# Loading a head's query weights as 88 and 40 partitions instead of 128

## The chip, the core and the metric

The kernel runs on one core of one Trainium2 chip. The metric is device time of one execution in microseconds (us). The core has TensorE (PE), VectorE (DVE), ScalarE (ACT), GpSimd (POOL) and a SyncE queue (SP), and 16 DMA engines that move data between HBM and the on-chip memory of 128 partitions.

## What is computed

One layer of a streaming encoder for 512 prompt frames and 32 sample frames of width 1024: RMSNorm, a projection, retention and a gated convolution, an output projection, and then PEER, a layer of single-neuron experts. In PEER, each of 8 heads asks for 16 of 16384 experts for every frame:

```
qry = (xb @ peer_query).reshape(P, PEER_HEADS, 2, PEER_KEY_DIM)
scores = einsum('phsd,hsnd->phsn', qry, keys)       # 128 keys in each of two halves
top_s, top_i = top_k(scores, 16)                    # then the best 16 of 16 x 16 sums
expert = (ia * PEER_KEYS + ib)                      # 16 experts a frame and head
u_rows = peer_down[expert]; v_rows = peer_up[expert]
act = gelu(einsum('pd,ped->pe', xb, u_rows))
out = einsum('pe,ped->pd', gate * act, v_rows)
```

The rows of `peer_down` and `peer_up` lie side by side in one table, `experts`, of 8 KB a row. The outputs are the final-normed frames and the retention and convolution states.

## The kernel before, in words

Everything is float32. The first 340 us hold the mixers (projection, convolution, retention); after them, and partly beside them, runs the PEER part, to which this change belongs.

PEER is cut into 34 steps, `vt`: four tiles of 128 frames for each of 8 heads, and two last steps in which the 32 sample frames are folded over the 128 partitions. Each step has 16 gathers, 544 in all. A gather (L601) is an indirect DMA that POOL issues: for each of 128 partitions one row of 8 KB, 1 MB in all, into one of 12 slots of `arena`. DVE waits for the slot's semaphore and takes the dot product of the first half of the rows with the frame (L1313); ACT makes of it the gelu and the weight (L895, L898) and a diagonal matrix (L909); PE multiplies the second half of the rows by it and sums in PSUM (L1674, for the sample L1667). When PE has used a slot, POOL may issue the gather that comes 12 later. So two things can hold the stream: the DMA engines, and the ring of 12 slots through DVE, ACT and PE.

Every gather's semaphore reaches its full count only when all DMA engines that carry a part of it have told of the end of theirs.

The weights of a head are 128 partitions of 2304 floats (queries and sub-keys), 1152 KB. They lie in two buffers in turn, `head_flat[head % 2]`, each with a semaphore (`s_hw`). Heads 0 and 1 are loaded earlier (L480, L491). A loop on SP loads heads 2 to 7 (L502 to L504): for head 2 it waits for PE's last scores of head 0, for each later one for the projections two heads back. PE asks for them in `later_query` (L1633), about one head before the head's own gathers. The order of work on each engine is written out; no scheduler is involved.

Of the kernel before, what the change touches and what calls it, by code (L numbers as in the profile page):

```python
# [14 lines left out]
P = 128  # L15
# [42 lines left out]
def shape_constants():  # L58

    f = np.float32  # L60
    half = HD // 2
    inv = (f(10000.0) ** (-np.arange(half, dtype=f) / f(half))).astype(f)
    pos = np.concatenate([np.arange(SEQ, dtype=f), f(PAST) + np.arange(DEC, dtype=f)])
    ang = (pos[:, None] * inv[None, :]).astype(f).astype(np.float64)
    trig = np.zeros((P, TILES, 2, half), f)
    for t in range(TILES):
        r = ROWS[t]
        trig[:r, t, 0] = np.cos(ang[t * P:t * P + r])
        trig[:r, t, 1] = np.sin(ang[t * P:t * P + r])
    log_gamma = np.log1p(-np.exp2(-5.0 - np.arange(HEADS)))  # L70
    i = np.arange(P)
    diff = i[None, :] - i[:, None]
    scale = HD ** -0.5
    decay = np.zeros((P, HEADS, P), f)
    cross = np.zeros((P, HEADS, P), f)
    key_decay = np.zeros((P, 2, HEADS), f)
    for h in range(HEADS):
        decay[:, h] = np.where(diff >= 0, np.exp(log_gamma[h] * np.maximum(diff, 0)), 0.0) * scale
        cross[:, h] = np.exp(log_gamma[h] * (i + 1.0))[None, :]
        key_decay[:, 0, h] = np.exp(log_gamma[h] * (P - 1.0 - i)) * scale  # L80
        key_decay[:DEC, 1, h] = np.exp(log_gamma[h] * (DEC - 1.0 - i[:DEC])) * scale
    ident = np.eye(P, dtype=f)
    fold = (np.arange(P)[:, None] % DEC == np.arange(P)[None, :]).astype(f)
    iota = np.broadcast_to(np.arange(TOPK, dtype=f), (P, TOPK))
    parts = [trig.reshape(P, -1), decay.reshape(P, -1), cross.reshape(P, -1), key_decay.reshape(P, -1),
             ident, fold, iota]
    return np.concatenate(parts, axis=1).astype(f)
# [33 lines left out]
def plan():  # L121
# [34 lines left out]
    def glu(s, *parts):  # L156
        return [("glu", s, c, i) for c, i in parts]
# [22 lines left out]
def parts(vt):  # L180

    steps = [range(g * GROUP, (g + 1) * GROUP) for g in range(GROUPS)]
    return steps if vt < VT - 1 else steps[:-1] + [range(k, k + 1) for k in steps[-1]]

def named(text):
# [39 lines left out]
def steps(vt, g):  # L226

    rows = parts(vt)[g]
    return [rows[i:i + 2] for i in range(0, len(rows), 2)]
# [9 lines left out]
def build(nc, x_prompt, x_sample, x_turned, state_ret, conv_state, weights, head_weights, params, consts, gain_ffn, gain_final,  # L239
          experts, y_prompt, y_sample, ret_prompt, ret_sample, conv_prompt, conv_sample):  # L240
    ctx = ExitStack()
    with ctx:
# [3 lines left out]
        def sem(name):  # L246
            return ctx.enter_context(nc.semaphore(name))
# [33 lines left out]
        head_flat = [region_b[:, first_at:first_at + HEAD_W + 2 * KEYS], region_b[:, 0:HEAD_W + 2 * KEYS]]  # L281
# [92 lines left out]
        s_hw = [sem("s_hw_even"), sem("s_hw_odd")]  # L374
# [59 lines left out]
        def _(sp):  # L434
# [64 lines left out]
            for head in range(2, PH):  # L499
                if head == 2:  # L500
                    sp.wait_ge(s_pe, JOB[("scores", SAMPLE)] + 1)
                else:  # L502
                    sp.wait_ge(s_proj, (head - 2) * PROJ)
                sp.dma_start(head_flat[head % 2], head_weights[head]).then_inc(s_hw[head % 2], 16)  # L504
            last = VT * TOPK - 1
            sp.wait_ge(s_slot[SLOT[last]], slot_filled(last))
            for t in range(SAMPLE):
# [965 lines left out]
        def _(pe):  # L1473
# [149 lines left out]
            def later_query(head, i):  # L1623

                weights = head_w[head % 2][0]
                if head == 1:
                    before = BEFORE_QUERIES[i]
                    pe.wait_ge(s_by[BY[before[0]]], EMPTIED[before])
                elif i < 3:
                    pe.wait_ge(s_scored, (head - 2) * 3 + (i + 1))  # L1630
                else:
                    pe.wait_ge(s_queries, (head - 1) * PIECES)
                pe.wait_ge(s_hw[head % 2], 16 * (head // 2 + 1))  # L1633
                s, half = i // 2, i % 2
                for k in range(KD):
                    last = mm(ps[:, Q_BANKS + i, 0:HALF], weights[:, k, s * KEYS:(s + 1) * KEYS],  # L1636
                              hT[:, k, half * HALF:(half + 1) * HALF], start=k == 0, stop=k == KD - 1)
                last.then_inc(s_proj, 1)
# [48 lines left out]
            def next_head(head, m):  # L1687

                if m == 0:
                    return {g: lambda g=g: later_query(head + 1, g) for g in range(PIECES)}  # L1690
                if m == 1:
                    return {2: lambda: later_scores(head + 1)}
                return {}

            for step in PLAN:
# [29 lines left out]
                else:  # L1725
                    sum_up(step[1], step[2])

            later_query(1, 0)
            later_query(1, 1)
            sum_up(2, 0)  # L1730
            later_query(1, 2)
# [81 lines left out]
```

## Time and profile before

| | us |
|---|---|
| median of 3 runs | 1667.71 (1667.13 to 1667.92) |
| the profiled execution | 1667.42 |
| its span, first to last instruction | 1665.6 |
| DVE busy | 1225.5 |
| PE busy | 1109.6 |
| POOL busy | 680.6 |
| ACT busy | 572.6 |
| SP loads of heads 2 to 7, issued | 344.0 to 1006.6 |

The profile's page gives busy times, the span in 40 slices, the DMA queues (q0 is POOL's, q1 SP's, q8 and q14 carry instructions), and the chain of work that ended last. The timeline gives single instructions with the idle time before them in brackets and what ended it. No view tells the 16 DMA engines apart.

### The profile page before, as it was taken

What the parts mean: (1) busy time and instruction counts of PE and PEld (TensorE: products, weight loads), DVE (VectorE), ACT (ScalarE), POOL (GpSimd) and SP (SyncE); (2) the same over time, 40 slices, a digit from 0 to 9 for tenths busy, and PEclk for the clock granted to TensorE, in tenths of its full rate; (3) what the DMA queues carried; (4) which work ended last, traced back from release to release, by engine and by line L of the source; (5) the groups of instructions that cost most, each with busy time, mean ns of one, the idle gap of its engine ahead of it and who ended that gap; (6) DMA issues with size and microseconds to landing.
All of it is one profiled execution on the core that took longest, in us unless ns stands there. A gap on an engine that the chain in (4) does not pass through costs nothing.

```text
span 1665.6 us, 19298 instructions
## 1 busy us (share of the span) xinstructions
PE 1109.6 (67%) x6327; PEld 464.1 (28%) x6327; DVE 1225.5 (74%) x2651; ACT 572.6 (34%) x1785; POOL 680.6 (41%) x633
## 2 busy tenths in 40 slices
PE   7999999785675567556654665567667656665533
PEld 6744465441231122112211221122113211111111
DVE  3997858976877777677767777777777777777755
ACT  2212232532333333333333333334333333333342
POOL 0004634544443444444344433444444444444552
PEclk9999999887897778877978887798768876767755
DMA  7203227999999999999999999999999999999995
GB/s 292 102 1 98 111 83 293 371 420 421 421 421 421 421 421 422 421 421 420 421 421 422 421 420 421 421 420 422 419 417 419 420 416 421 419 417 419 420 421 239
DMA packets 88004, 608.73 MB, mean 365 GB/s; under 512 B 11104, under 2 KB 13664, under 8 KB 16224
## 3 DMA queue, kind: packets, MB, share of 16 engines
q0 software_dynamic: 78336, 570.46, 82.8%
q1 hardware_dynamic: 9568, 37.04, 6.0%
q8 instruction: 50, 0.82, 0.2%
q14 instruction: 50, 0.41, 0.1%
HBM read 604.19 MB, written 2.88 MB: 364 GB/s over the span
## 4 chain that ended last, share of the span: by engine, by line
DMA 47%; PE 23%; DVE 17%; issue 5%; POOL 4%; DVEq 2%; ACT 2%; ACTq 0%; SPq 0%; POOLq 0%
DMA arena<-experts,expert 46%; PE ps L1536 8%; PE ps L1674 8%; DVE arena L1313 7%; PE ps L1516 4%; POOL arena L601 4%; DVE xs L1334 4%; DVEq L1250 1%; ACT late L909 1%; DVE rot_tmp L1273 1%; DVE codes L1251 1%; ACT weight L898 1%; DVE top_s L1254 1%; DVE top_s L1249 1%; PE ps L1495 1%
## 5 line engine op out<-in xcount | busy, mean ns | idle before, releaser
L1674 PE MATMUL ps<-arena,late 64*64 64x512 f32 x4032 | 663.5, 799 | 480.6 <-ACT late L909 480.4
L601 POOL DMA_INDIRECT arena<-experts,expert x544 | 609.0, 1119 | 772.8 <-PE ps L1674 648.5
L1313 DVE CUSTOM_DVE_ANT_0 arena<-arena,hn 128x1024 f32<-128x1024 f32 x544 | 651.0, 1222 | 311.0 <-DMA arena<-experts,expert 307.4
L1674 PEld LDWEIGHTS ps<-arena,late 64*64 64x64 f32 x4032 | 173.9, 172 | 944.0 <-ACT late L909 696.3
L895 ACT ACTIVATE gl<-dots 128x2 f32<-128x2 f32 (+1 forms) x274 | 55.8, 204 | 810.3 <-DVE dots L1313 810.3
L909 ACT ACTIVATE late<-cst,weight 128x128 f32<-128x128 f32 (+1 forms) x536 | 183.6, 389 | 18.9 <-issue 0.3
L898 ACT ACTIVATE weight<-gl,gate 128x1 f32<-128x1 f32 x544 | 130.8, 287 | 19.5 <-issue 0.7
L1536 PE MATMUL ps<-arena,hT 128*128 128x512 f32 x256 | 111.1, 593 | 0.0
L1636 PE MATMUL ps<-hT,region_b 128*128 128x272 f32 x448 | 110.8, 401 | 0.0
L1064 DVE SCALAR_TENSOR_TENSOR region_b<-region_b,par 128x574 f32<-128x574 f32 x120 | 92.6, 813 | 4.5
L1636 PEld LDWEIGHTS ps<-hT,region_b 128*128 128x128 f32 x448 | 83.8, 192 | 39.3 <-issue 23.5
L1334 DVE TENSOR_TENSOR xs<-ps,xs 64x512 f32<-64x512 f32 x128 | 88.0, 688 | 2.3
L1536 PEld LDWEIGHTS ps<-arena,hT 128*128 128x128 f32 x256 | 48.2, 190 | 58.1 <-issue 58.1
L1667 PE MATMUL ps<-arena,late 128*32 128x256 f32 x256 | 30.1, 611 | 47.8 <-ACT late L909 47.8
L1536 PE MATMUL ps<-arena,region_b 128*128 128x512 f32 x128 | 56.5, 595 | 2.5 <-issue 2.5
L551 POOL TENSOR_TENSOR rot_tmp<-arena,cst 128x512 f32<-128x512 f32 (+1 forms) x5 | 6.3, 1266 | 125.4 <-DVE hn L1212 125.0
L1313 DVE DVE_READ_ACCUMULATOR2_ANT dots<- 128x1 f32 x544 | 44.8, 82 | 0.0
L871 ACT ACT_TABLE_LOAD x33 | 42.3, 1283 | 1.7
L895 ACT ACT_TABLE_LOAD x32 | 41.1, 1283 | 0.6
L1516 PE MATMUL ps<-hn,arena 128*128 128x272 f32 x160 | 36.8, 392 | 0.0
L1536 PEld LDWEIGHTS ps<-arena,region_b 128*128 128x128 f32 x128 | 23.8, 190 | 31.0 <-issue 30.9
L1516 PEld LDWEIGHTS ps<-hn,arena 128*128 128x128 f32 x160 | 30.4, 190 | 6.3
(174 smaller groups left out, 853.4 us busy)
## 6 DMA issues: line engine op xcount, KB each, us to landing
arena<-weights SPq DMA_DIRECT2D x6, 2048.0 KB, 10.9
region_b<-head_weights SPq DMA_DIRECT2D x8, 1152.0 KB, 9.4
arena<-experts,expert POOLq DMA_INDIRECT x544, 23.0
hT<-x_turned SPq DMA_DIRECT2D x2, 1088.0 KB, 7.2
arena<-weights SPq DMA_DIRECT2D x4, 512.0 KB, 10.7
xs<-x_prompt SPq DMA_DIRECT2D x4, 512.0 KB, 10.0
arena<-weights SPq DMA_DIRECT2D x2, 1024.0 KB, 13.8
y_prompt<-xs SPq DMA_DIRECT2D x4, 512.0 KB, 3.8
```

Of the source, the lines that this page charges most:

```text
L601: pool.indirect_dma_start(rows_of(n), None, experts, bass.IndirectOffsetOnAxis(ap=expert[:, vt % BUFS, k:k + 1], axis=0))\
L871: nc.scalar.activation(gate[:, u, :], best_s[:, u, :], ACT.Exp, bias=neg_max[:, u:u + 1], accum_out=gate_sum[:, u:u + 1]).then_inc(s_exp, 1)
L895: nc.scalar.activation(gl[:, vt % 2, ks], dots[:, vt % 2, ks], ACT.Gelu_apprx_tanh)
L898: ready = nc.scalar.activation(weight[:, vt % 2, k:k + 1], gl[:, vt % 2, k:k + 1], ACT.Copy, scale=gate[:, vt % BUFS, k:k + 1])
L909: nc.scalar.activation(diag[:, n % DIAGS, 0:base.shape[-1]], base, ACT.Copy, scale=weight[:, vt % 2, k:k + 1])\
L1064: return v.scalar_tensor_tensor(out=conv[:, c, :], in0=u[:, c, j:j + WIDE], scalar=gain, in1=conv[:, c, :], op0=ALU.mult, op1=ALU.add)
L1313: last = v.tensor_tensor_reduce(out=rows_of(n)[:, 0:D], in0=rows_of(n)[:, 0:D], in1=hn[:, tile_of(vt)], scale=1.0, scalar=0.0, op0=ALU.mul ...
L1334: last = v.tensor_tensor(out=part, in0=total, in1=part, op=ALU.add)
L1516: last = mm(out[:, 0:HALF], w[:, c, k, :], columns[:, k, i * HALF:(i + 1) * HALF], start=k == 0, stop=k == KD - 1)
L1536: last = mm(out, lhs[:, k, lo:lo + r], w[:, k, :], start=k == 0, stop=k == KD - 1)
L1636: last = mm(ps[:, Q_BANKS + i, 0:HALF], weights[:, k, s * KEYS:(s + 1) * KEYS], hT[:, k, half * HALF:(half + 1) * HALF], start=k == 0, sto ...
L1674: last = mm(ps[half * TOKENS:(half + 1) * TOKENS, 2 * (vt % 2) + i, :], diag[tokens, n % DIAGS, tokens], rows_of(n)[tokens, D + half * SEC ...
```

## The change

A list of partition ranges per head is put in: heads 2, 3 and 4 have two, 0 to 87 and 88 to 127, all others one. SP issues one transfer for each range, and the wait of PE counts 16 for each. The same bytes go to the same places.

```diff
+def head_rows(head):
+
+    return [slice(0, 88), slice(88, P)] if 2 <= head < 5 else [slice(0, P)]
+
+
+def head_filled(head):
+
+    return 16 * sum(len(head_rows(h)) for h in range(head % 2, head + 1, 2))
...
-                sp.dma_start(head_flat[head % 2], head_weights[head]).then_inc(s_hw[head % 2], 16)
+                for rows in head_rows(head):
+                    sp.dma_start(head_flat[head % 2][rows], head_weights[head][rows]).then_inc(s_hw[head % 2], 16)
...
-                pe.wait_ge(s_hw[head % 2], 16 * (head // 2 + 1))
+                pe.wait_ge(s_hw[head % 2], head_filled(head))
```

On SP's queue, from the copies of the sample frames to the stores of the output, this stood before (the size is partitions x floats):

```order
L494 DMA hn<-hn 32x1024 [waits s_hn]
L494 DMA hn<-hn 32x1024 x2
L495 DMA region_b<-gain_final 128x1024
L497 DMA var<-gain_final 32x256 x4
L504 DMA region_b<-head_weights 128x2304 [waits s_pe]
L504 DMA region_b<-head_weights 128x2304 [waits s_proj] x5
L509 DMA y_prompt<-xs 128x1024 [waits s_yout,s_slot7]
```

And this stands there now:

```order
L504 DMA hn<-hn 32x1024 [waits s_hn]
L504 DMA hn<-hn 32x1024 x2
L505 DMA region_b<-gain_final 128x1024
L507 DMA var<-gain_final 32x256 x4
L515 DMA region_b<-head_weights 88x2304 [waits s_pe]
L515 DMA region_b<-head_weights 40x2304
L515 DMA region_b<-head_weights 88x2304 [waits s_proj]
L515 DMA region_b<-head_weights 40x2304
L515 DMA region_b<-head_weights 88x2304 [waits s_proj]
L515 DMA region_b<-head_weights 40x2304
L515 DMA region_b<-head_weights 128x2304 [waits s_proj] x3
L520 DMA y_prompt<-xs 128x1024 [waits s_yout,s_slot7]
```

Three transfers have become six, each second one issued right behind its first; the waits stand where they stood. On PE, DVE, ACT and POOL every instruction keeps its place.

## Rows read from the trace of the kernel before

**Rows 1.** The page: span, DVE, the 40 slices of DMA, the queues.

```profile
span 1665.6 us, 19298 instructions
...
DVE  3997858976877777677767777777777777777755
...
DMA  7203227999999999999999999999999999999995
GB/s 292 102 1 98 111 83 293 371 420 421 421 421 421 421 421 422 421 421 420 421 421 422 421 420 421 421 420 422 419 417 419 420 416 421 419 417 419 420 421 239
...
q0 software_dynamic: 78336, 570.46, 82.8%
...
q8 instruction: 50, 0.82, 0.2%
q14 instruction: 50, 0.41, 0.1%
```

**Rows 2.** The page's chain that ended last, by engine.

```profile
DMA 47%; PE 23%; DVE 17%; issue 5%; POOL 4%; DVEq 2%; ACT 2%; ACTq 0%; SPq 0%; POOLq 0%
```

**Rows 3.** All waits: who waited for whom, us, times, the longest.

```profile
POOL arena L601 <- PE ps L1674: 648.5, 314, 8.3
...
DVE arena L1313 <- DMA arena<-experts,expert: 307.4, 247, 3.7
```

**Rows 4.** DMA issues: count, KB each, median us from issue to landing.

```profile
region_b<-head_weights SPq DMA_DIRECT2D x8, 1152.0 KB, 9.4
arena<-experts,expert POOLq DMA_INDIRECT x544, 23.0
```

**Rows 5.** Timeline of DVE near 1056 us: start, duration, instruction, [idle before].

```profile
1053.58 1.23 DVE L1313 CUSTOM_DVE_ANT_0 arena<-arena,hn 128x1024 f32<-128x1024 f32 x1 [1.19 <-DMA arena<-experts,expert]
...
1056.06 1.23 DVE L1313 CUSTOM_DVE_ANT_0 arena<-arena,hn 128x1024 f32<-128x1024 f32 x1 [1.25 <-DMA arena<-experts,expert]
...
1058.54 1.23 DVE L1313 CUSTOM_DVE_ANT_0 arena<-arena,hn 128x1024 f32<-128x1024 f32 x1 [1.25 <-DMA arena<-experts,expert]
```

**Rows 6.** Timeline of DVE, five dot products around the longer steps.

```profile
492.17 1.23 DVE L1313 CUSTOM_DVE_ANT_0 arena<-arena,hn 128x1024 f32<-128x1024 f32 x1 [2.28 <-DMA arena<-experts,expert]
...
1105.72 1.23 DVE L1313 CUSTOM_DVE_ANT_0 arena<-arena,hn 128x1024 f32<-128x1024 f32 x1 [0.89 <-DMA arena<-experts,expert]
...
1109.18 1.23 DVE L1313 CUSTOM_DVE_ANT_0 arena<-arena,hn 128x1024 f32<-128x1024 f32 x1 [2.22 <-DMA arena<-experts,expert]
...
1230.32 1.23 DVE L1313 CUSTOM_DVE_ANT_0 arena<-arena,hn 128x1024 f32<-128x1024 f32 x1 [2.23 <-DMA arena<-experts,expert]
...
1583.80 1.23 DVE L1313 CUSTOM_DVE_ANT_0 arena<-arena,hn 128x1024 f32<-128x1024 f32 x1 [2.26 <-DMA arena<-experts,expert]
```

**Rows 7.** Timeline of DVE while the weights of head 5 come in.

```profile
679.15 1.23 DVE L1313 CUSTOM_DVE_ANT_0 arena<-arena,hn 128x1024 f32<-128x1024 f32 x1 [0.28 <-DMA arena<-experts,expert]
...
683.02 1.22 DVE L1313 CUSTOM_DVE_ANT_0 arena<-arena,hn 128x1024 f32<-128x1024 f32 x1 [2.56 <-DMA arena<-experts,expert]
...
686.90 1.23 DVE L1313 CUSTOM_DVE_ANT_0 arena<-arena,hn 128x1024 f32<-128x1024 f32 x1 [2.65 <-DMA arena<-experts,expert]
...
689.39 1.23 DVE L1313 CUSTOM_DVE_ANT_0 arena<-arena,hn 128x1024 f32<-128x1024 f32 x1 [1.25 <-DMA arena<-experts,expert]
```

**Rows 8.** Windows: stretch, length, busy of each engine, clock, DMA share, GB/s.

```profile
430.00:1180.00 750.00, 465.83 (x2772) 169.81 (x2768) 555.07 (x1271) 272.37 (x879) 322.13 (x294) 0.82 1.01 421
...
1240.00:1480.00 240.00, 152.59 (x852) 50.10 (x856) 179.24 (x410) 88.46 (x284) 106.33 (x96) 0.76 1.01 419
```

**Rows 9.** Timeline of SP: loads of heads 2, 3, 4; of PE: head 2's first projection.

```profile
344.02 0.35 SPq L504 DMA_DIRECT2D region_b<-head_weights  x1
...
378.51 0.35 SPq L504 DMA_DIRECT2D region_b<-head_weights  x1
...
512.55 0.33 SPq L504 DMA_DIRECT2D region_b<-head_weights  x1
...
450.88 3.93 PE L1636 MATMUL ps<-hT,region_b 128*128 128x272 f32 x16
```

## The prediction, made before the changed kernel was run

> **What bounds the kernel now.** Start with the page. The 40 slices show the DMA engines full from slice 7 or 8 on, at some 420 GB/s in every slice up to the last, while DVE stays near seven tenths [rows 1]. The chain that ended last is DMA for 47% [rows 2]. The waits seem to say something else: POOL waits 648.5 us for PE to free a slot, DVE only 307.4 us for gathers [rows 3]. The issues settle it. A gather lands 23.0 us after its issue [rows 4], and one lands every 2.48 us (next paragraph), so about nine lie queued at the DMA engines at any time. POOL's waits are idle time behind a full queue. The queue is the bound.
>
> Now the timeline of DVE, because where a dot product waited for its gather, its start marks the landing. Near 1056 us the starts are 2.48 us apart, each with over 1 us of waiting [rows 5]. 1 MB (1,048,576 B) in 2.483 us is 422 GB/s, the rate of the slices. But a landing is told only when the last of 16 DMA engines has done its part, so this clock shows the latest engine, not the mean one. And it hiccups: from 1105.72 to 1109.18 is 3.46 us, 0.98 more than 2.48 [rows 6]. From 1109.18 to 1230.32 is 121.14 us, which is 48 steps of 2.483 and two times 0.98: one hiccup each 60.6 us. The first in the rows is at 492.17, the last at 1583.80, 1091.6 us later, so 18 periods and 19 hiccups, 18.6 us together.
>
> Does every DMA engine lose these 0.98 us, or only one? If all did, the stream would move 24 gathers in 60.6 us, 415 GB/s. The window from 430 to 1180 us shows 421, from 1240 to 1480 us 419 [rows 8]. So the other engines run ahead, and one engine is late alone, later by 0.98 at each hiccup. That the rate falls after 1200 us fits too: by then the others are so far ahead that the ring of 12 slots stops them now and then. Who is last decides: its queue never runs dry, so the end of the stream is the end of all bytes laid on that one engine.
>
> **The change, part by part.** Nothing moves on PE, DVE, ACT and POOL. SP issues three transfers more, at 0.33 to 0.35 us each [rows 9]; behind them on SP stands only the wait for the next head, over 30 us away, so they cost nothing. The wait of PE counts 16 more for each. Head 2 is issued at 344.02 and first needed at 450.88 [rows 9]; its load takes 9.4 us [rows 4]. Even at twice that some 85 us of cover stay, and PE has gathers to sum meanwhile. Nothing there either.
>
> What is left is how a load weighs on the DMA engines. It weighs on the stream directly: around the load of head 5 the steps are 3.87, 3.88 and then 2.49 us [rows 7]; 7.75 less two plain steps of 2.48 is 2.79 us. That is also 1152 KB at 422 GB/s. Spread evenly over 16 engines this is 8 rows (partitions) an engine, 0.349 us a row.
>
> The changed transfers have 88 and 40 rows. All SP transfers in the DMA list that bear on this stretch have 128 or 32 rows, multiples of 16, so the trace does not show what becomes of others. Two ways bound it. (a) All 16 engines take part, some with one row more: 5 or 6 of the 88 and 2 or 3 of the 40. An engine then has 7 to 9 rows instead of 8, 0.35 us either way for a head, 1.05 us for three. (b) Only equal shares of whole rows are made: 88 as 11 times 8 and 40 as 10 times 4, the largest divisors not over 16. If both count from the same end, ten engines have 12 rows, one has 8, and five have none. An engine with none saves 2.79 us a head, 8.37 us for heads 2 to 4; one with 12 rows loses 4 x 0.349 = 1.40 a head, 4.19 us for the three.
>
> I take (b). The Trainium skill states it so ("DMA: Bandwidth & Descriptors", section on why a DMA increments its semaphore by 16): a transfer goes over the largest number of engines up to 16 that divides its outer dimension, on SP's queue the lowest-numbered ones. No row here shows it. Without that page (a) and (b) would be bounds of equal right.
>
> Then the sum. If the late engine is one of the five, it loses 8.37 us of work, and the end moves by that unless another engine becomes last. The swing against an engine with 12 rows is 8.37 + 4.19 = 12.6 us. The late engine's private load is the 18.6 us of hiccups. Let x be what the heaviest of the ten carries of the same kind. The gain is the smaller of 8.37 and 18.6 - 4.19 - x = 14.4 - x. For x there is a mean: the packets of q8 and q14 took 0.3% of 16 engines' span, 0.003 x 16 x 1665.6 = 80 us; less 19 for the late one, 61 us over 15 engines, 4.1 us each [rows 1]. Up to x = 6.0 the gain is full. From the profiled 1667.42 us (its span of 1665.6 and 1.8 around it) this gives 1659.0. The median of the runs lies 0.3 us above the profiled one, so 1659.3 us.
>
> Is the late engine among the five? That is the weakest step, because no view numbers the engines. By count it would be 5 in 16. I go higher: its hiccups are regular, one private stream, and the large q8 stream (0.82 MB, twice q14's) must mostly go elsewhere. An order that fills engines from the first on would leave a private stream at the far end. I hold 2 in 3, as a judgement, no more.
>
> The Trainium skill ("DMA: Bandwidth & Descriptors", section on latency and other measured facts) calls engines 7 and 15 usually slower than the rest. The trace agrees that a single engine lags, by 0.98 us each 60.6. By this page it is 15, which is spared, or 7, which gets 12 rows: 1659.3 or 1671.9.
>
> **The rivals.** First, another engine is close behind. The same mechanism, but one of the ten has x = 9 instead of 4, for instance a second private stream. The gain is 14.4 - 9 = 5.4 us: 1662.3. For it speaks that the 61 us need not lie evenly; against it nothing in the rows.
>
> Second, nothing changes. Either (a) holds, or the late engine is the one with 8 rows, or x is over 14: within 1 us of 1667.7. For (a) speaks only the plain look of the thing: same bytes, same count of engines. The Trainium skill has a rule against such splits (same page, rules for kernel authors: two transfers to disjoint partition halves go over the same engines, so use one of 128 partitions). By it the change would bring nothing, 1667.7. It speaks of halves, 64 rows each, which are multiples of 16; 88 and 40 are not.
>
> Third, slower. The late engine is one of the ten with 12 rows. It is last before and after, nothing can cover it, and each of three loads costs 1.40 us more: 1667.7 + 4.2 = 1671.9. This holds from the first load that finds it last. By count of engines this is 10 in 16; it is the same question as above, answered the other way.
>
> **How the numbers follow.** Full gain 0.42; a close second 0.23; nothing 0.11; slower 0.24. The predicted time is the first, 1659.3 us. Its own range is 1658.3 to 1660.5, from the spread of the runs (0.8 us) and the rounding of the steps. Since the fourth case holds more than 2 in 10, the range has to reach it: 1658.5 to 1672.1. A change of 0.2% (3.3 us) is about what a measurement of this kernel can tell from none. Faster by more than that are the first case and most of the second: 0.64. Slower is the fourth: 0.24. Within it the rest: 0.12.
>
> **What would show it.** In the timeline of DVE after the change:
> - Around the loads of heads 3 and 4 (380 and 515 us) the extra over 2.48 us steps sums to 4.2 us for each head, if an engine with 12 rows is then last. If it is 2.8, the shares are even and (a) holds.
> - The 0.98 us hiccups each 60.6 us are gone from the landings after 520 us, until late, if the late engine was spared. If they stand where they stood, it was not, and the time is about 1672.
> - If other hiccups take their place, with a period of their own, the close second is last, and its period gives x.
> - The slices' GB/s from 430 us on stay at 420 or above for longer; a rate of 417 early would mean that the ring of slots stops the spared engines and the swing is partly lost.
> - PE's first projection of heads 2 to 4 must not wait for a load.
>
> The forecast is wrong if the time lies over 1661, and its mechanism is wrong if the steps at the loads of heads 3 and 4 are those of before.

## The result: 21.4 us slower

| | median us | runs |
|---|---|---|
| before | 1667.82 | 1667.13 to 1670.07 |
| changed | 1689.24 | 1688.89 to 1689.78 |

The ratio is 1.0126, with a 95% interval of 1.0109 to 1.0144. The prediction was 1659.3 us with a range up to 1672.1: wrong in sign, and the slowest rival, 1671.9, is far exceeded too. The profiled execution took 1689.78 us, its span 1688.0.

The page of the changed kernel, lines that answer to [rows 1]:

```profile
span 1688.0 us, 19301 instructions
...
DVE  3997758964875777677767777777777777777755
...
GB/s 288 100 1 120 87 115 271 390 361 363 421 421 361 415 420 421 421 418 419 421 421 419 420 421 419 421 417 422 412 421 417 421 416 414 422 413 414 419 420 245
DMA packets 88019, 608.73 MB, mean 361 GB/s; under 512 B 11119, under 2 KB 13679, under 8 KB 16239
```

Slices 8, 9 and 12 (338 to 422 us, and 506 to 549) fell from 420 to some 361 GB/s. They hold the three split loads. A slice is 42.2 us, so 59 GB/s less is 2.5 MB less, 5.9 us of the full stream for each slice, 17.8 us for the three, and some of a load's loss lies in slice 13 (415) too. Between them and after them the stream is nearly as it was (slices 10 and 11 both read 421, as before; slices 28 to 38 are lower by 2 GB/s on average). The same line of the page before:

```profile
DMA packets 88004, 608.73 MB, mean 365 GB/s; under 512 B 11104, under 2 KB 13664, under 8 KB 16224
```

The bytes are equal, and 15 small packets were added. In the traces' records of single packets, which no view prints, each transfer from SP has a packet of 4 bytes for each DMA engine that carries it: cols2 below has three transfers of 128 rows more and 48 such packets more, 16 each. Here 3 x (11 + 10) instead of 3 x 16 is 15 more. So the reading (b) of the prediction, 88 over 11 engines and 40 over 10, is what the chip does. The trace agrees with the Trainium skill ("DMA: Bandwidth & Descriptors", section on why a DMA increments its semaphore by 16) on how many engines carry a transfer. Which ones they are, no run here shows.

What a split load does to the landings, in the timeline of DVE at head 3 of the changed kernel (SP issued it at 387.85 us):

```profile
390.77 1.23 DVE L1324 CUSTOM_DVE_ANT_0 arena<-arena,hn 128x1024 f32<-128x1024 f32 x1 [1.24 <-DMA arena<-experts,expert]
...
397.60 1.23 DVE L1324 CUSTOM_DVE_ANT_0 arena<-arena,hn 128x1024 f32<-128x1024 f32 x1 [5.59 <-DMA arena<-experts,expert]
...
405.86 1.23 DVE L1324 CUSTOM_DVE_ANT_0 arena<-arena,hn 128x1024 f32<-128x1024 f32 x1 [7.03 <-DMA arena<-experts,expert]
...
408.33 1.22 DVE L1324 CUSTOM_DVE_ANT_0 arena<-arena,hn 128x1024 f32<-128x1024 f32 x1 [1.24 <-DMA arena<-experts,expert]
```

The steps are 6.83, 8.26 and 2.47 us. Over two plain steps of 2.48 that is 10.1 us, where an unsplit load cost 2.79 [rows 7]. The prediction named 4.2 for an engine with 12 rows. The windows around the same load show more (start:end, length, busy of PE, PEld, DVE, ACT, POOL, clock, DMA share, GB/s), first the changed kernel:

```profile
385.00:391.00 6.00, 4.86 (x48) 2.99 (x44) 2.69 (x5) 2.33 (x10) 4.48 (x6) 1.00 1.01 419
391.00:405.00 14.00, 5.48 (x32) 1.15 (x28) 2.24 (x4) 2.73 (x10) 3.95 (x5) 0.75 1.02 252
405.00:411.00 6.00, 0.13 (x4) 0.13 (x8) 3.68 (x12) 1.27 (x5) 0.39 (x1) 0.50 1.00 411
```

and the kernel before, around its load of head 3:

```profile
376.00:382.00 6.00, 4.36 (x40) 2.82 (x36) 3.21 (x6) 1.58 (x6) 4.78 (x5) 1.00 1.01 422
382.00:388.00 6.00, 1.95 (x16) 0.51 (x16) 1.23 (x2) 2.45 (x8) 2.73 (x3) 1.00 1.01 422
```

Before, a load shares the full 422 GB/s with the gathers. Now the rate falls to 252 GB/s for 14 us, while the DMA share stays at 1.02: the DMA engines are not idle, their packets take longer. The packet records show it directly, over the three loads together:

| run | weight packet (9216 B), mean ns | gather packet (8192 B) during a load, mean ns |
|---|---|---|
| before | 353 | 312 |
| changed | 570 | 549 |

Elsewhere between 400 and 1150 us a gather packet takes 315 ns in the changed kernel and 314 in the one before. The gathers bear most of it: q0's packets took 82.8% of 1665.6 us before and 82.5% of 1688.0 now, some 13 us more for each engine, q1's some 5. Uneven shares alone would have left each packet as long as it was. So the engines stand in each other's way, and this was in no case of the prediction.

Loads that are not split cost what they did. At head 5 the steps are 3.87, 3.89 and 2.47 us, as in [rows 7]:

```profile
701.46 1.23 DVE L1324 CUSTOM_DVE_ANT_0 arena<-arena,hn 128x1024 f32<-128x1024 f32 x1 [0.33 <-DMA arena<-experts,expert]
...
705.33 1.23 DVE L1324 CUSTOM_DVE_ANT_0 arena<-arena,hn 128x1024 f32<-128x1024 f32 x1 [2.57 <-DMA arena<-experts,expert]
...
709.22 1.23 DVE L1324 CUSTOM_DVE_ANT_0 arena<-arena,hn 128x1024 f32<-128x1024 f32 x1 [2.65 <-DMA arena<-experts,expert]
...
711.69 1.22 DVE L1324 CUSTOM_DVE_ANT_0 arena<-arena,hn 128x1024 f32<-128x1024 f32 x1 [1.24 <-DMA arena<-experts,expert]
```

And the late engine was not spared. Its hiccup, the step that is 0.98 us longer each 60.6 us, is still in the landings after the three split loads:

```profile
634.96 1.23 DVE L1324 CUSTOM_DVE_ANT_0 arena<-arena,hn 128x1024 f32<-128x1024 f32 x1 [0.91 <-DMA arena<-experts,expert]
...
638.39 1.23 DVE L1324 CUSTOM_DVE_ANT_0 arena<-arena,hn 128x1024 f32<-128x1024 f32 x1 [2.20 <-DMA arena<-experts,expert]
```

This step is 3.43 us, 0.95 over 2.48, and from 638.39 to 701.46 are 63.07 us, 25 steps of 2.483 and 0.99. An engine freed of three loads while ten others got more would lie over 12 us ahead at this point and would not be seen in the landings. It is the same hiccup as before: in both kernels a gather packet of 968 ns lies beside a packet of 8 KB on q14, at 614.9 us before and at 636.9 now, both some 137 gathers into the stream.

### The profile page after: what moved, and what is told of

It reads as the page before. It is cut to its first block, busy times and chain, and to the rows that moved or that the text cites. A ratio compares the mean times of both kernels' runs of the same rounds, so it can differ in the third digit from the quotient of the medians.

```text
span 1688.0 us, 19301 instructions
## 1 busy us (share of the span) xinstructions
PE 1103.8 (65%) x6327; PEld 461.2 (27%) x6327; DVE 1226.5 (73%) x2651; ACT 572.5 (34%) x1785; POOL 681.8 (40%) x633
## 3 DMA queue, kind: packets, MB, share of 16 engines
q0 software_dynamic: 78336, 570.46, 82.5%
## 4 chain that ended last, share of the span: by engine, by line
DMA 47%; PE 22%; DVE 17%; issue 5%; POOL 4%; DVEq 2%; ACT 2%; ACTq 0%; SPq 0%; POOLq 0%
DMA arena<-experts,expert 47%; PE ps L1547 8%; PE ps L1685 7%; DVE arena L1324 7%; POOL arena L612 4%; PE ps L1527 4%; DVE xs L1345 4%; DVEq L1261 1%; ACT late L920 1%; DVE rot_tmp L1284 1%; DVE codes L1262 1%; PE ps L1506 1%; ACT weight L909 1%; PE ps L1544 1%; DVE top_s L1265 1%
```

## The experiments

All edits are made to the changed kernel's `head_rows` or its loop. "Over" is the median less that of the kernel before on the same chip, divided by the number of heads cut (three, for head2_only one). The first runs weigh three theories. A is placement: what costs is that the DMA engines write other partitions than in a 128-row transfer. B is the second transfer as such. C is that fewer engines carry the load. Where partitions are left out the results are wrong, and with the scores the gathers of these heads fetch other experts; between 560 and 830 us the stream ran at 421 GB/s all the same in both half_32_95 and half_0_63, as before.

| run | partitions of each transfer | median us | before us | over, us a head | small packets over 11104 |
|---|---|---|---|---|---|
| changed | 88, 40 | 1689.24 | 1667.82 | 7.1 | 15 |
| cols2 | 128, 128 (half rows) | 1668.42 | 1668.24 | 0.1 | 48 |
| rows64 | 64, 64 | 1681.28 | 1668.24 | 4.3 | 48 |
| rows112_16 | 112, 16 | 1678.93 | 1668.24 | 3.6 | 48 |
| head2_only | 88, 40 (one head) | 1675.06 | 1668.24 | 6.8 | 5 |
| rows120_8 | 120, 8 | 1684.61 | 1668.08 | 5.5 | 21 |
| half_32_95 | 64 (half left out) | 1663.61 | 1668.08 | -1.5 | 0 |
| half_0_63 | 64 (half left out) | 1670.43 | 1668.08 | 0.8 | 0 |
| rows32_64_32 | 32, 64, 32 | 1674.69 | 1668.66 | 2.0 | 96 |
| rows4x32 | 32 four times | 1682.71 | 1668.66 | 4.7 | 144 |
| only88 | 88 (40 left out) | 1678.41 | 1668.66 | 3.2 | -15 |
| only40 | 40 (88 left out) | 1673.01 | 1668.66 | 1.4 | -18 |

The small packets agree with equal shares in every run: 120 and 8 partitions add 3 x (15 + 8 - 16) = 21, and 88 alone take 3 x (16 - 11) = 15 away.

**cols2: two transfers of all partitions.**

```diff
-    return [slice(0, 88), slice(88, P)] if 2 <= head < 5 else [slice(0, P)]
+    width = HEAD_W + 2 * KEYS
+    return [slice(0, width // 2), slice(width // 2, width)] if 2 <= head < 5 else [slice(0, width)]
...
-                    sp.dma_start(head_flat[head % 2][rows], head_weights[head][rows]).then_inc(s_hw[head % 2], 16)
+                    sp.dma_start(head_flat[head % 2][:, rows], head_weights[head][:, rows]).then_inc(s_hw[head % 2], 16)
```

> The loads of heads 2 to 4 are cut in two along the row instead: two transfers of 128 partitions and 4.6 KB a partition. The changed kernel takes 21.4 us more than the one before, 7.1 us for each split load. Theory A (placement): what costs is that with 88 and 40 rows a DMA engine writes other partitions than it writes in a 128-row transfer and in the gathers; here all stay with 128 rows, so the time is that of before, 1667 to 1669 us. Theory B (a second transfer costs): each split costs some 7 us whatever its shape, so 1689 us. Theory C (fewer engines: 11 and 10 carry it, since the trace of the changed kernel has 15 small packets more, 21 instead of 16 for each of three loads): 128 rows go over 16 engines, so 1667 to 1669 us.

Measured 1668.42 us, ratio 0.9998 (0.9988 to 1.0007). A second transfer costs nothing that can be told from the spread of the runs. Theory B falls.

**rows64: 64 and 64 partitions.**

```diff
-    return [slice(0, 88), slice(88, P)] if 2 <= head < 5 else [slice(0, P)]
+    return [slice(0, 64), slice(64, P)] if 2 <= head < 5 else [slice(0, P)]
```

> The loads of heads 2 to 4 are cut into 64 and 64 partitions. Both are multiples of 16, so all 16 engines carry 4 rows of each and 8 in sum, as before. Theory A (placement): an engine takes 4 neighbouring partitions of a half instead of its own 8, so both halves crowd on the partitions that half of the engines write in the gathers; slower than before, by at least half of the 21.4 us: over 1678 us. Theory B (a second transfer costs): 1689 us. Theory C (fewer engines): nothing is uneven, so 1667 to 1669 us.

Measured 1681.28 us, ratio 1.0076 (1.0059 to 1.0093). All 16 engines have 8 rows, and yet more than half of the loss is there. Theory C, fewer engines, can't be the main cause. During the load of head 3 the rate falls to 299 GB/s:

```profile
391.00:405.00 14.00, 4.36 (x28) 0.95 (x20) 3.29 (x7) 1.99 (x8) 3.77 (x4) 0.76 1.01 299
```

**rows112_16: 112 and 16 partitions.**

```diff
-    return [slice(0, 88), slice(88, P)] if 2 <= head < 5 else [slice(0, P)]
+    return [slice(0, 112), slice(112, P)] if 2 <= head < 5 else [slice(0, P)]
```

> The loads of heads 2 to 4 are cut into 112 and 16 partitions, 7 rows and 1 row for each of 16 engines, 8 in sum as before. Theory A (placement): the 7 neighbouring rows of an engine are not the ones it writes in the gathers; slower, 1675 to 1690 us. Theory B (a second transfer costs): 1689 us. Theory C (fewer engines): 1667 to 1669 us.

Measured 1678.93 us, ratio 1.0068 (1.0051 to 1.0085). Again even in rows and slower, as theory A has it.

**head2_only.**

```diff
-    return [slice(0, 88), slice(88, P)] if 2 <= head < 5 else [slice(0, P)]
+    return [slice(0, 88), slice(88, P)] if head == 2 else [slice(0, P)]
```

> Only head 2 is cut into 88 and 40 partitions; heads 3 and 4 are loaded in one transfer as before. All theories in which each split load costs the stream the same, as the late engine was last at all three: a third of 21.4 us, so 1667.8 + 7.1 = 1674.9 us. If the loss needs the lags of several loads to add up before the ring of 12 slots runs dry, the first alone costs clearly less: under 1671 us.

Measured 1675.06 us, ratio 1.0040 (1.0026 to 1.0055): 6.8 us for one head, where 7.1 was expected. Each split load costs by itself.

**half_32_95 and half_0_63: the same shape in two places.** The rest of the partitions of heads 2 to 4 is not loaded.

```diff
-    return [slice(0, 88), slice(88, P)] if 2 <= head < 5 else [slice(0, P)]
+    return [slice(32, 96)] if 2 <= head < 5 else [slice(0, P)]
```

 Theory A (placement): half the bytes and no crossing, so the stream gains half of 2.79 us a head: 1668.2 - 4.2 = 1664.0 us. Theory D (any shape that is not of 128 rows is slow, wherever it lies): the same time as with partitions 0 to 63, 1669 to 1671 us. Theory C (fewer engines): 1664.0 us.

```diff
-    return [slice(0, 88), slice(88, P)] if 2 <= head < 5 else [slice(0, P)]
+    return [slice(0, 64)] if 2 <= head < 5 else [slice(0, P)]
```

 Two halves of this kind cost 13.0 us over an unsplit load for three heads (1681.28 against 1668.24), so one costs half: 1668.2 + 6.5 = 1674.7, less the 8.4 us of bytes that are not loaded twice over: between 1668.2 - 4.2 + 2 and 1674.7, taken as (1681.28 + 1668.24 - 8.4) / 2 = 1670.6 us. Theory C (fewer engines): 1664.0 us, as with 32 to 95. Theory D: 1670.6 us, and the same for 32 to 95.

Measured 1663.61 us, ratio 0.9968 (0.9956 to 0.9979), and 1670.43 us, ratio 1.0013 (1.0003 to 1.0023). As many rows, as many bytes, 16 engines in both; only which partitions they are differs, and 6.8 us lie between them. This pair settles that the place counts. The timeline of DVE at the load of head 3, with partitions 32 to 95:

```profile
382.97 1.23 DVE L1324 CUSTOM_DVE_ANT_0 arena<-arena,hn 128x1024 f32<-128x1024 f32 x1 [1.24 <-DMA arena<-experts,expert]
...
386.84 1.23 DVE L1324 CUSTOM_DVE_ANT_0 arena<-arena,hn 128x1024 f32<-128x1024 f32 x1 [2.64 <-DMA arena<-experts,expert]
...
389.33 1.23 DVE L1324 CUSTOM_DVE_ANT_0 arena<-arena,hn 128x1024 f32<-128x1024 f32 x1 [1.26 <-DMA arena<-experts,expert]
```

and with partitions 0 to 63:

```profile
389.11 1.23 DVE L1324 CUSTOM_DVE_ANT_0 arena<-arena,hn 128x1024 f32<-128x1024 f32 x1 [1.25 <-DMA arena<-experts,expert]
...
395.23 1.23 DVE L1324 CUSTOM_DVE_ANT_0 arena<-arena,hn 128x1024 f32<-128x1024 f32 x1 [4.88 <-DMA arena<-experts,expert]
...
397.70 1.23 DVE L1324 CUSTOM_DVE_ANT_0 arena<-arena,hn 128x1024 f32<-128x1024 f32 x1 [1.25 <-DMA arena<-experts,expert]
```

The first step is 3.87 us, 1.39 over 2.48, exactly half of 2.79. The second is 6.12, 3.64 over: half the bytes cost more than the whole did. The choice of 32 to 95 came from the Trainium skill ("SBUF — State Buffer", the section on door 1, the DMA port swizzle: partitions fall into 16 groups of eight, each with a port of its own; bits 4 to 2 and bit 6 of the partition's number pick it). The trace agrees: 1.39 against 3.64 us. By this grouping 32 to 95 lie on all 16 groups, four rows each, and 0 to 63 on eight groups, eight rows each.

The windows over the two loads of head 3, first partitions 32 to 95, then 0 to 63:

```profile
384.00:388.00 4.00, 0.99 (x12) 0.11 (x4) 1.36 (x4) 0.56 (x3) 1.88 (x2) 1.00 1.01 420
389.00:394.00 5.00, 2.35 (x12) 0.73 (x16) 1.23 (x2) 1.38 (x5) 1.86 (x2) 0.78 1.01 233
```

A weight packet took 353 ns in the first and 580 in the second (medians 353 and 618), a gather packet beside it 313 and 529. One rival was not tested: the two runs also read other rows of the weights in HBM. Against it speaks that the gathers' packets, which read another table, were slowed as well.

**rows120_8.**

```diff
-    return [slice(0, 88), slice(88, P)] if 2 <= head < 5 else [slice(0, P)]
+    return [slice(0, 120), slice(120, P)] if 2 <= head < 5 else [slice(0, P)]
```

> The loads of heads 2 to 4 are cut into 120 and 8 partitions: 8 rows on each of 15 engines and 1 on each of 8, if equal shares are made. The most loaded engine has 9 rows instead of 12 with 88 and 40. Theory A with unevenness on top: placement costs what it costs in 112 and 16, 10.7 us, and 0.35 us a head for the ninth row: 1668.2 + 10.7 + 1.0 = 1680 us. If the number of engines that carry the load is what counts and not their rows, it lies near the changed kernel, 1687 to 1689 us.

Measured 1684.61 us, ratio 1.0099 (1.0082 to 1.0116). That is between the two expectations, 4.6 over the first. The rows on the fullest engine alone do not set the cost: with 8 rows it is 0.1 us a head in cols2, 3.6 in rows112_16 and 4.3 in rows64.

**head0_split: a load with no gather beside it.** Head 0 is loaded at 164 us, among other SP loads of 128 rows.

```diff
-    return [slice(0, 88), slice(88, P)] if 2 <= head < 5 else [slice(0, P)]
+    return [slice(0, 88), slice(88, P)] if head == 0 else [slice(0, P)]
...
-            sp.dma_start(head_flat[0], head_weights[0]).then_inc(s_hw[0], 16)
+            for rows in head_rows(0):
+                sp.dma_start(head_flat[0][rows], head_weights[0][rows]).then_inc(s_hw[0], 16)
```

> Only the load of head 0 is cut into 88 and 40 partitions; it comes at 164 us, when no gather is under way, between loads of SP alone. In the kernel before it lands 7.7 us after its issue. Theory A in the form that only the crossing with the gathers' own writes costs: it lands within 2 us of that, and the total stays at 1667 to 1669 us. Theory A in the form that the engines of the split transfer crowd each other as well: it lands 4 to 8 us later, 12 to 16 us after the issue; nobody waits for it before 218 us, so the total is 1667 to 1669 us all the same.

One run, 1668.42 us. The windows of the kernel before:

```profile
165.00:170.00 5.00, 5.00 (x17) 2.51 (x16) 4.70 (x5) 0.00 (x0) 4.72 (x5) 1.00 0.96 391
170.00:175.00 5.00, 5.00 (x19) 2.71 (x18) 4.91 (x4) 2.92 (x4) 4.82 (x4) 1.00 0.95 409
175.00:180.00 5.00, 5.00 (x13) 2.18 (x12) 4.77 (x4) 0.00 (x0) 4.71 (x5) 1.00 0.07 29
```

and of this run:

```profile
165.00:170.00 5.00, 5.00 (x19) 2.69 (x18) 4.78 (x4) 0.00 (x0) 4.86 (x4) 1.00 1.00 305
170.00:175.00 5.00, 5.00 (x19) 2.76 (x18) 4.83 (x5) 2.92 (x4) 4.68 (x5) 1.00 1.08 222
175.00:180.00 5.00, 5.00 (x14) 2.13 (x13) 4.78 (x4) 0.00 (x0) 4.71 (x5) 1.00 0.81 197
```

What was all but done by 175 us now goes on at 197 GB/s until 180. The trace's landing events put the load's end 14.8 us after its issue (164.86 to 179.64), 7.7 before (164.28 to 171.96). These 7.1 us are as long as the loss of a split load in the stream. So the loss does not need the gathers: the engines of the split transfer crowd each other, or the other SP loads beside it, which this single run does not tell apart. Nobody waits for this load, and the total stays.

**Theory E, put to four runs.** A group takes one row in 0.349 us, whoever brings it, and a transfer goes at the pace of its fullest group. Its addition of 0.75 us for each misplaced transfer was fitted to the runs so far.

```diff
-    return [slice(0, 88), slice(88, P)] if 2 <= head < 5 else [slice(0, P)]
+    return [slice(0, 32), slice(32, 96), slice(96, P)] if 2 <= head < 5 else [slice(0, P)]
```

> The loads of heads 2 to 4 are cut into partitions 0 to 31, 32 to 95 and 96 to 127: three transfers, 8 rows an engine in sum. Theory E counts rows in groups of partitions: the 16 groups are those that the engines of a 128-row transfer keep to, a group takes one row in 0.349 us whoever brings it, and the transfer goes at the pace of its fullest group; on top come 0.75 us for each transfer that leaves its engines' own groups (half_0_63 against a full load). By E the runs so far come out, over an unsplit load and for one head, as 64+64: 2.79 + 1.5 = 4.3 (measured 4.3), 88+40: 5.59 + 1.5 = 7.1 (7.1), 112+16: 1.75 + 1.5 = 3.3 (3.6), 120+8: 4.19 + 1.5 = 5.7 (5.5). Here: 32 rows on 8 groups take 1.40 us each time and the middle 64 on 16 groups 1.40, in sum 4.19, 1.40 over 2.79, and 2 x 0.75: 2.9 us a head, 1668.1 + 8.7 = 1676.8 us. Theory F: each row brought to another's group costs the same, 4.35/64 = 0.068 us; here some 60 rows, 4.1 us a head: 1680.3 us. A cost for each further transfer instead (3.6 us): 1689 us.

Measured 1674.69 us, ratio 1.0035 (1.0022 to 1.0047).

```diff
+    return [slice(i, i + 32) for i in range(0, P, 32)] if 2 <= head < 5 else [slice(0, P)]
```

> The loads of heads 2 to 4 are cut into four transfers of 32 partitions, each 2 rows an engine. Theory E: four times 1.40 us on 8 of 16 groups, 5.58, which is 2.79 over the unsplit load, and 4 x 0.75: 5.8 us a head, 1668.1 + 17.4 = 1685.5 us. Theory F: some 124 rows brought to other groups, 8.4 us a head: 1693 us. A cost for each further transfer (3.6 us): 1700 us.

Measured 1682.71 us, ratio 1.0078 (1.0061 to 1.0096). In both E is nearest, F and a fixed cost for each transfer are far off. But E misses too, by 2.1 and 2.8 us, and its addition of 0.75 us for each misplaced transfer is too much: over the groups' pace remain 0.3 us for each of two and 0.5 us for each of four.

```diff
+    return [slice(0, 88)] if 2 <= head < 5 else [slice(0, P)]
```

> Only partitions 0 to 87 of heads 2 to 4 are loaded; 88 to 127 are left out. Theory E: eight engines at a time bring rows to four groups, 8 steps of 2 x 0.349, 5.58 us, which is 2.79 over the full load, and 0.75: 3.5 us a head, 1668.1 + 10.6 = 1678.7 us. If only the number of rows on the most loaded engine counted, it has 8 as before: 1668.1 us.

Measured 1678.41 us, ratio 1.0054 (1.0037 to 1.0070): E's time within 0.3 us, and its extra over the kernel before within 0.9 (9.8 for 10.6). The groups' totals alone would not give it: no group gets more than 8 of these 88 rows, as in a full load.

```diff
+    return [slice(88, P)] if 2 <= head < 5 else [slice(0, P)]
```

> Only partitions 88 to 127 of heads 2 to 4 are loaded; 0 to 87 are left out. Theory E: ten engines bring 4 rows each, two groups get 8: 2.79 us, as the full load, and 0.75: 1668.1 + 2.2 = 1670.3 us. Rows on the most loaded engine alone: 4 instead of 8, 1668.1 - 4.2 = 1663.9 us.

Measured 1673.01 us, ratio 1.0025 (1.0015 to 1.0035): a miss by 2.7 us for E, and by 9 us for a count of rows on engines. 40 rows alone, a third of the bytes, cost 1.4 us a head more than all 128 in one transfer. Both parts add up: 3.25 + 1.45, and 2.79 because the unsplit load is taken off in both, make 7.5 us, near the 7.1 of the change.

Counted for every run, with each engine taking neighbouring partitions and all of them going through their shares in step, the groups' pace gives this, in us a head over an unsplit load:

| run | counted | measured |
|---|---|---|
| half_32_95 | -1.4 | -1.5 |
| cols2 | 0 | 0.1 |
| half_0_63 | 0 | 0.8 |
| only40 | 0 | 1.4 |
| rows32_64_32 | 1.4 | 2.0 |
| only88 | 2.8 | 3.2 |
| rows64 | 2.8 | 4.3 |
| rows4x32 | 2.8 | 4.7 |
| rows112_16 | 3.5 | 3.6 |
| rows120_8 | 4.2 | 5.5 |
| changed | 5.6 | 7.1 |

For rows112_16 the expectation of rows32_64_32 has 1.75, which is too low by this count: 112 rows take 7 x 2 and 16 rows 4 turns of 0.349 us, 6.3 in sum. But for 0.1 us at half_32_95 the count never lies above what was measured, and it puts the runs nearly in order. What it leaves, 0 to 1.9 us, follows no rule that these runs show.

## Why the prediction was wrong

**What bounds the kernel: right.** The DMA stream and the last landing were the bound. half_32_95 shows it best: half of three loads taken off gave 4.5 us, where 3 x 1.39 = 4.2 was to be had.

**SP's issues, PE's wait, the cover of the loads: right.** PE's first projection of head 2 ran at 464.45 us, over 100 us after the load, and waited for nothing:

```profile
464.45 3.94 PE L1647 MATMUL ps<-hT,region_b 128*128 128x272 f32 x16
```

cols2, with as many transfers and issues, is at 1668.42.

**Equal shares over 11 and 10 engines, reading (b): right**, by the 15 small packets.

**"One with 12 rows loses 4 x 0.349 = 1.40 a head": this step failed.** It let each DMA engine run at its own speed and counted only its rows. The split loads cost 7.1 us a head instead. 0.349 us a row was read from a 128-row load, whose packets of a row took 353 ns; in the split loads they took 570.

**"Is the late engine among the five? I hold 2 in 3": wrong as well**, by the hiccups that stayed. This alone would have made it the third rival, 1671.9 us. That rival had the sign and a fifth of the size, and its mechanism, rows on the fullest engine, is not what cost the time. The gain of 8.37 us for a spared engine could not show here, since the late engine was not spared.

**The rule weighed against the change.** The prediction set aside the advice of the Trainium skill ("DMA: Bandwidth & Descriptors", rules for kernel authors) to use one 128-partition transfer, with the words that it speaks of halves, multiples of 16. rows64 is such a pair of halves and costs 13.0 us. The advice holds, and for more than its reason there (the halves go over the same engines, so nothing is won): here they lose.

No run beat the kernel before with all its work done.

## What to carry to other kernels

When the DMA engines are full, a transfer's price is not its bytes alone but where each engine writes. In this kernel an SP load of 128 partitions could be split along the row for nothing, while each cut by partitions cost 2.0 to 7.1 us a load, even where all 16 engines got equal shares. A price per row that was read from one shape was here a bound from below for the others, and a range should say so.

## What the runs showed that was not expected

- 64 rows on partitions 32 to 95 cost 1.39 us of the stream, on 0 to 63 3.64 us. Packets of the same size took 353 ns in the one and 580 in the other.
- A split load slowed the gathers more than itself in sum: their packets took 549 ns instead of 312 while it ran.
- While a load was cut by partitions, the core's DMA rate fell from 422 to 252 GB/s, with the DMA share still at 1.02. A full DMA share does not mean full bandwidth; the GB/s must be read beside it.
- The DMA engine that is 0.98 us later each 60.6 us stayed the last one through three split loads.
